# Two token tiles leave the dense dots for fetched rows of a turned u; GpSimd makes u's second half part

## What is computed

```python
s1 = jnp.einsum('thd,kd->thk', qh[:, :, 0], peer_keys1)
s2 = jnp.einsum('thd,kd->thk', qh[:, :, 1], peer_keys2)
v1, i1 = lax.top_k(s1, PEER_TOPK)
v2, i2 = lax.top_k(s2, PEER_TOPK)
cand = (v1[..., :, None] + v2[..., None, :]).reshape(-1, PEER_HEADS, PEER_TOPK * PEER_TOPK)
vals, flat = lax.top_k(cand, PEER_TOPK)
e = i1[flat // 16] * PEER_KEYS + i2[flat % 16]
g = jax.nn.softmax(vals, axis=-1)
act = jax.nn.gelu(jnp.einsum('thkd,td->thk', peer_u[e], xb))
out = jnp.einsum('thk,thkd->td', g * act, peer_v[e])
```

## Time and profile before

| | |
|---|---|
| median of 3 runs | 4723.21 us |
| the profiled execution, its span | 4720.1 us |
| TensorE (matmul) busy | 4462.5 us, 95% |
| VectorE busy | 2881.6 us, 61% |
| ScalarE busy | 1338.1 us, 28% |
| GpSimd busy | 913.8 us, 19% |
| dense dots, busy | 1454.0 us, 9216 matmuls |
| sums, busy | 1085.1 us, 6144 matmuls |
| projections, busy | 493.0 us, 3168 matmuls |
| mean granted TensorE clock | 0.965 of 2.4 GHz |

### The profile page before, as it was taken

The page is one execution under the profiler, slowest core; times in us unless marked ns, Lnnn a source line. Parts: engine busy times, 40 slices in busy tenths (PEclk is TensorE's granted clock), DMA queues, the critical chain, the costliest instruction groups (busy, mean ns, idle before and its releaser), DMA issues. The chain is left out here.

```text
span 4720.1 us, 71047 instructions
## 1 busy us (share of the span) xinstructions
PE 4462.5 (95%) x26288; PEld 2684.0 (57%) x26288; DVE 2881.6 (61%) x5144; ACT 1338.1 (28%) x1823; POOL 913.8 (19%) x982
## 2 busy tenths in 40 slices
PE   6999988999888997999999999999996999999997
PEld 2666643444555665666666666666663555555554
DVE  4456413444865454256667666665536888888885
ACT  3223213333211003224444444443222222222221
POOL 0000103322000110000000000000005656666650
PEclk8999989999978998999999999999998999999998
DMA  4543523331545562245554555555438888888881
GB/s 184 177 149 128 181 58 94 85 86 45 162 137 207 204 212 89 77 148 180 189 192 171 201 191 183 182 200 182 151 119 308 301 297 293 300 293 299 291 289 48
DMA packets 398289, 859.52 MB, mean 182 GB/s; under 512 B 42626, under 2 KB 233730, under 8 KB 389186
## 3 DMA queue, kind: packets, MB, share of 16 engines
q1 hardware_dynamic: 274786, 474.82, 30.1%
q0 software_dynamic: 78752, 283.31, 17.7%
q10 hardware_dynamic: 44480, 97.93, 5.5%
HBM read 677.90 MB, written 178.03 MB: 181 GB/s over the span
## 5 line engine op out<-in xcount | busy, mean ns | idle before, releaser
L381 PE MATMUL dot_ps<-h_parts,u_parts 128*128 128x384 f16 (+1 forms) x9216 | 1454.0, 317 | 7.9 <-PEq L2050 5.4
L381 PEld LDWEIGHTS dot_ps<-h_parts,u_parts 128*128 128x128 f16 x9216 | 893.1, 98 | 499.6 <-issue 8.6
L381 PE MATMUL totals_ps<-act_parts,v_parts 128*128 128x416 f16 x6144 | 1085.1, 340 | 36.8 <-DVE act_parts L3010 28.8
L381 PEld LDWEIGHTS totals_ps<-act_parts,v_parts 128*128 128x128 f16 x6144 | 602.1, 98 | 518.5 <-issue 33.4
L394 PE MATMUL in_ps<-h_parts_in,in_parts 128*128 128x384 f16 (+1 forms) x3168 | 493.0, 318 | 4.7 <-DVE in_parts L721 4.5
L2686 DVE SCALAR_TENSOR_TENSOR u_parts<-u_chunks,units,u_parts 128x1024 f16<-128x1024 f32 x126 | 161.8, 1284 | 517.6 <-ACT u_parts L2470 517.6
L2479 ACT ACTIVATE gelu<-dot_ps,units 128x384 f32<-128x384 f32 (+1 forms) x384 | 216.3, 564 | 804.1 <-PE dot_ps L381 803.6
L394 PEld LDWEIGHTS in_ps<-h_parts_in,in_parts 128*128 128x128 f16 x3168 | 309.4, 98 | 182.3 <-DVE in_parts L721 4.6
L3097 POOL DMA_INDIRECT row_value<-tmp_g_rows,row_g x256 | 305.2, 1192 | 394.0 <-POOLq L2344 316.2
L2945 ACT ACTIVATE v_parts<-v_group,units 128x1024 f16<-128x1024 f32 x128 | 136.9, 1138 | 772.7 <-PE totals_ps L381 740.1
L3104 POOL DMA_INDIRECT rows_in<-in_v,row_v x204 | 285.8, 1401 | 229.9 <-DVE row_sums L3040 98.5
(11 more groups left out here) (371 smaller groups left out, 5294.2 us busy)
## 6 DMA issues: line engine op xcount, KB each, us to landing
u_chunks<-in_u SPq DMA_DIRECT2D x128, 512.0 KB, 5.6
v_sweep<-in_v SPq DMA_DIRECT2D x128, 512.0 KB, 4.7
v_group<-in_v SPq DMA_DIRECT2D x31, 2048.0 KB, 8.4
tmp_g<-gelu ACTq DMA_DIRECT2D x128, 416.0 KB, 2.7
tmp_w<-h POOLq DMA_DIRECT2D x26, 2048.0 KB, 8.1
w_groups<-tmp_w SPq DMA_DIRECT2D x32, 1664.0 KB, 11.7
gelu_in<-tmp_g SPq DMA_DIRECT2D x31, 1664.0 KB, 8.9
merge_sweep<-in_u POOLq DMA_DIRECT2D x64, 512.0 KB, 7.8
```

Of the source, the lines that this page charges most:

```text
L381: mm = pe.matmul(bank, left(x), right(y), start=first and x == 0 and y == 0, stop=last and x == 1)
```

## The change

1. The last 256 tokens (two blocks of 128) leave the dense dots; these now run over 832 tokens in two parts of 416 (DSPLITS), in two PSUM banks.
2. For them u is needed with an expert's 1024 values in one row. While u chunks lie in the sweep buffers of the projections (64) and of the join (64), TensorE turns each by eight transposes (two fills of four, class Turned), ScalarE copies a fill from PSUM and stores the rows to tmp_u_rows. The projections have one bank for fills and the ring of two; the join two banks and a ring of four, with a query weight chunk in a ring of its own.
3. In the dots GpSimd fetches 256 times a row of u for each of 128 tokens (a ring of four), and VectorE multiplies it with the token's h and sums along it in one instruction; h of the two blocks is turned by 16 transposes at the start. At the end one gelu and one product make the coefficients, so g_rows, its 256 value fetches and their products go.
4. The second f16 part of u moves to GpSimd, as a plain subtraction; for that ScalarE scales the f32 chunk in place with a second instruction.
5. The expert choice for the two blocks starts in the queries (the first 16 of each key half, ten searches per query chunk); their tiles come first. 128 chunks are now 8 ahead, 16 more, 6 turns of 16, 8 behind, and the last 16 one-hot groups run beside the last 8.
6. The maxima of v move: 64 into the projections, 36 beside the v product, 28 into the queries. Stores of w move from GpSimd's queue to ScalarE's.

```diff
+class Turned:
+    FILLS = 2
+    def __init__(self, nc, ctx, sem, name, a, s, sweep, banks):
+        self.a, self.s, self.sweep, self.banks = a, s, sweep, banks
+        self.rows = ctx.enter_context(nc.sbuf_tensor(name + "_rows", [P, 2, D], F32))
+        self.turned, self.taken = sem(name + "_turned"), sem(name + "_turn_taken")
+        self.stored = [sem(f"{name}_rows_out{r}") for r in range(2)]
+    def load(self, pool, n, src):
+        if n >= self.sweep.ring:
+            pool.wait_ge(self.turned, (n - self.sweep.ring + 1) * self.FILLS)
+        self.sweep.load(pool, n, src)
+    def tensor(self, pe, turn, per, k, fill):
+        at = k * self.FILLS + fill
+        if fill == 0:
+            self.sweep.wait_loaded(pe, turn, per, k)
+        pe.wait_ge(self.taken, turn * (per * self.FILLS) + at + 1)
+        bank = self.banks[at % len(self.banks)]
+        src = self.sweep.buf[k % self.sweep.ring]
+        for j in range(4):
+            col = (fill * 4 + j) * P
+            mm = pe.transpose(bank[:, j * P:(j + 1) * P], src[:, col:col + P], self.s["const"][:, C_ID:C_ID + P])
+        mm.then_inc(self.turned, 1)
+    def scalar(self, act, turn, per, k, fill, first=0):
+        at, slot = k * self.FILLS + fill, k % 2
+        if fill == 0:
+            act.wait_ge(self.stored[slot], turn * (16 * per // 2) + 16 * (k // 2 + 1))
+        act.wait_ge(self.turned, turn * (per * self.FILLS) + at + 1)
+        act.copy(self.rows[:, slot, fill * 512:(fill + 1) * 512],
+                 self.banks[at % len(self.banks)]).then_inc(self.taken, 1)
...
+        LATE_SWEEP = CH_G // RING - CH_X // RING
+        sweep = Sweep(nc, ctx, sem, "proj", s["u_tops"], 2, [s["rstd"][:, 0:KC * P]])
+        v_sweep = Sweep(nc, ctx, sem, "proj_v", s["v_tops"], 2)
+        to_rows = Turned(nc, ctx, sem, "proj", a, s, sweep, [ps_v[:, :]])
         with nc.Block() as block:
             @block.gpsimd
             def _(pool):
-                sweep.gpsimd(pool)
+                for n in range(SWEPT):
+                    to_rows.load(pool, n, a["u"][n].rearrange("p k e -> p (k e)"))
+                    v_sweep.load(pool, n, a["v"][n // GRP, :, n % GRP, :])
+                for n in range(V_STEPS, V_STEPS + V_TAIL):
+                    v_sweep.load(pool, n, a["v"][n // GRP, :, n % GRP, :])
             @block.sync
             def _(sp):
...
+                            if swept is not None and k % 2 == 0:
+                                to_rows.tensor(pe, swept, PASS, 2 * u + k // 4, k // 2 % 2)
                         if u == 1 and not last:
                             scales.turn(pe, i + 1)
                         if u == 2 and not last:
...
-                def take(i, func, row0, dest, last=False):
-                    act.wait_ge(unit_ready, i + 1)
+                def take(i, func, row0, dest, swept, last=False):
                     for u in range(RING):
                         b = u % 2
+                        for f in range(2 * Turned.FILLS):
+                            to_rows.scalar(act, swept, PASS, 2 * u + f // 2, f % 2)
+                        if u == 0:
+                            act.wait_ge(unit_ready, i + 1)
...
+                def passing(swept, us, vs):
+                    for k in us:
+                        sweep.vector(dve, swept, PASS, k)
+                    for k in vs:
+                        v_sweep.vector(dve, swept, PASS, k)
                 def turn(i, work=None, swept=None):
                     set_unit(i)
                     found(i + 1)
                     if work:
                         work(0)
+                    if swept is not None:
+                        for k in range(4):
+                            passing(swept, (k,), (k,))
                     scales.powers(dve, link.link, i + 1)
                     if work:
                         work(1)
+                    if swept is not None:
+                        passing(swept, (4, 5), (4, 5))
                     take_scales(i + 1)
-                    for u in range(3):
-                        split(i + 1, u)
-                        if swept is not None:
-                            for k in range(2):
-                                sweep.vector(dve, swept, 2 * u + k)
+                    split(i + 1, 0)
+                    split(i + 1, 1)
+                    if swept is not None:
+                        passing(swept, (6,), ())
+                    split(i + 1, 2)
+                    if swept is not None:
+                        passing(swept, (7,), ())
                     if work:
                         work(2)
                     split(i + 1, 3)
                     if swept is not None:
-                        for k in range(2):
-                            sweep.vector(dve, swept, 6 + k)
+                        passing(swept, (), (6, 7))
                     if work:
                         work(3)
...
+                assert SWEPT == V_STEPS == (last + 1) * PASS
+                for k in range(PASS):
+                    passing(last, (k,), (k,))
                 for t in range(TILES + 1):
                     n = min(P, T - t * P)
...
                     dve.tensor_tensor(s["dt_tok"][0:n, t, :], ps_dt[0:n, 0:SH],
                                       s["par"][0:n, W_DTB:W_DTB + SH], ALU.add).then_inc(dt_taken, 1)
+                    for k in range(4):
+                        v_sweep.vector(dve, 0, PASS, V_STEPS + t * 4 + k)
...
-        EACH = 5
-        sweep = Sweep(nc, ctx, sem, "merge", a, s, SWEPT, NK - SWEPT, EACH, [], 2 * EACH, range(2 * EH))
+        PASS = 4
+        sweep = Sweep(nc, ctx, sem, "merge", s["u_tops"], PASS)
+        query_sweep = Sweep(nc, ctx, sem, "merge_query", s["u_tops"], 1)
+        turn_ps = ctx.enter_context(nc.psum_tensor("merge_turn_ps", [P, 2, 512], F32))
+        to_rows = Turned(nc, ctx, sem, "merge", a, s, sweep, [turn_ps[:, b, :] for b in range(2)])
         with nc.Block() as block:
             @block.gpsimd
             def _(pool):
-                sweep.gpsimd(pool)
+                for n in range(SWEPT):
+                    to_rows.load(pool, n, a["u"][SWEPT + n].rearrange("p k e -> p (k e)"))
+                    if n % PASS == PASS - 1:
+                        c = n // PASS
+                        query_sweep.load(pool, c, a["w_query"][c].rearrange("p k e -> p (k e)"))
...
+                def turn_fill(step, at):
+                    to_rows.tensor(pe, step, PASS, at // Turned.FILLS, at % Turned.FILLS)
                 group[0].tensor(pe)
                 group[1].tensor(pe)
                 pe.wait_ge(o_in, 16)
...
                                           start=(k == 0), stop=(k == NA - 1))
+                            turn_fill(i * 2 + u, j)
                         if u == 0:
                             pe.wait_ge(y_ready, KC)
                         for j, (t0, n) in enumerate(SPLITS):
                             for k in range(KC):
                                 mm = pe.matmul(ps[:, NS + j, 0:n], wb[:, u, k, :], y[:, k, t0:t0 + n],
                                                start=(k == 0), stop=(k == KC - 1))
+                                if k == 3:
+                                    turn_fill(i * 2 + u, NS + 2 * j)
                             mm.then_inc(br_done, 1)
+                            if j < NS - 1:
+                                turn_fill(i * 2 + u, NS + 2 * j + 1)
                 pe.wait_ge(br_taken, KC * NS)
...
                                                start=(k == 0), stop=(k == KC - 1))
+                                if k in (1, 4) or k == 6 and j < NS - 1:
+                                    turn_fill(i * 2 + (KC + u), 3 * j + (1, 4, 6).index(k))
                             mm.then_inc(mix_done, 1)
                 norm.tensor(pe)
...
+                        to_rows.scalar(act, i, PASS, at // Turned.FILLS, at % Turned.FILLS, SWEPT)
                 act.wait_ge(mix_taken, KC + 2)
                 norm.scalar(act)
                 shifted(act, s, h, 3 * KC, h_scaled)
+                to_rows.end(act, SWEPT)
             @block.vector
             def _(dve):
                 link = Chain(dve, chain)
...
+                def passing(step):
+                    for k in range(PASS):
+                        sweep.vector(dve, step, PASS, k, SWEPT)
+                    query_sweep.vector(dve, step, 1, 0, NK)
                 dve.sem_inc(mix_taken, 2)
                 for g in range(NG):
...
-                        for k in range(EACH):
-                            sweep.vector(dve, i, EACH * u + k)
+                        passing(i * 2 + u)
...
-                        for k in range(EACH):
-                            sweep.vector(dve, i + KC // 2, EACH * u + k)
+                        passing(i * 2 + (KC + u))
...
+                def rest(at):
+                    r = (at.n + 2) % 4
+                    pool.wait_ge(u_hi, at.chunk(off=3))
```

(36 more changed lines are left out.)

## The result

The changed kernel takes 4802.5 us, the median of four runs (4783.9 to 4807.5), against 4723.7 us of the kernel before beside it: 1.016 times as long, with an interval of 1.014 to 1.018. It is slower, as forecast. The time is 60 us above the predicted 4742, inside the range. A second set of four runs gave 4796.0 us (ratio 1.016, 1.014 to 1.018). The first profiled execution was the fastest of its set, 4783.9 us; that of the second set, 4796.4, is the typical one. Both are read here.

What follows compares the result with a forecast made beforehand. TensorE was taken to bound the projections, join, dots and sums. 4720.1 - 335 (dots) + 118 (transposes) + 62 (projections) + 24 (their end) + 109 (join) + 29 (clock) + 12 (small terms) = 4739; median 4742 us, range 4640 to 4870.

Steps and rivals of the forecast that it cites:

- Transposes +118: Projections and join: 256 fills of four transposes at 0.46 us add 118 us to TensorE, half in each.
- Join +109, clock apart: Join: TensorE waits for ring refills, 8.4 us at seven branch steps and 6.4 at eight output steps, 109 us.
- Rival 1: Projections and join: loads land in time, rings don't hold TensorE; 4542 us, 4645 with half the stalls; chance 0.20.
- Projections +62: Projections: new TensorE waits of 3.9, 2.3 and 0.9 us a turn, and 15 us in turn 7; sum 62 us.
- the clock: Half clock after TensorE stalls: 1.7 us a restart, 15 in the join and two in the projections, +29 us.
- Rival 3: Join: the clock stays low, two fifths of it at 1.2 GHz, +120 us, 4870 us; chance 0.08.
- End of the projections +24: After the input products: 36 v maxima through two slots, paced by landings at 3.14 us each, add 24 us.
- Dots -335: Dots: a chunk's dense matmuls fall from 11.03 to 8.41 us, over 128 chunks saving 335 us.
- VectorE: 114 of 150 us: Dots: VectorE's work per turn goes from 109 to 114 us, within a turn of 150 us.
- rival 4: Dots: VectorE's rows come late, a row product twice as dear, 154 of 150 us a turn; +40, 4790 us; chance 0.04.
- rival 2: Dots: GpSimd becomes the bound; 4790 us at 6 us a subtraction, 4980 at 8 us; chance 0.14.
- To the dots +4, to the sums +8: Small terms: token transposes 2 and VectorE's searches 2; end of the dots 4 and five row fetches 4 us.

Runs made afterwards that it cites:

- e1_join_first: The changed kernel with VectorE taking a step's five maxima ahead of its additions in the join, not behind: 4652.9 us, 0.985 of the kernel before.
- e3_v_ring4: The changed kernel with four slots instead of two in the projections' ring for v's chunks: 4759.3 us, 1.008 of the kernel before.
- e4_proj_order: The changed kernel with some u and v maxima moved earlier in VectorE's order in a projection turn: 4738.5 us, 1.003 of the kernel before.
- e6_vector_sub: The changed kernel with u's second part made by VectorE again in the dots, without GpSimd's subtraction and ScalarE's scaling in place: 4781.9 us.
- e8_old_pool_sub: The kernel before with only GpSimd's subtraction, ScalarE's scaling in place and w's stores on ScalarE's queue: 4729.0 us, ratio 1.0013.

## Why the prediction was right, and where its sizes were off

**What bounds the kernel, and the sign: right.** The ring of the join refilled behind the step (146 us) and the transposes (55 in the join, as many by estimate in the projections) take back 256 of the 310 us that the dense cut gave; the rest made it slower. `e1_join_first` shows the cause of the sign directly: with TensorE's waits in the join gone the change pays, which neither `e3_v_ring4` nor `e4_proj_order` reaches alone.

**Transposes +118.** 0.46 us a fill from the rows of another phase, 0.43 measured in the join: right. In the projections a fill wasn't measured by itself.

**Join +109, clock apart.** Measured 105.9 and 108.3, 15 times, 9.1 us the longest. The chain of the step (VectorE's order, issue, landing) was right in each link; the waits are 7.1 us each in the mean where 7.3 were forecast. Rival 1 (rings that don't hold TensorE) is out with them.

**Projections +62.** The sum of waits is 61.9 us (35.2 + 19.5 + 7.2), but its make-up is not that of the prediction. A turn has one wait of 5.1 to 6.4 us, not three of 3.9, 2.3 and 0.9: the load took 7.7 us to land instead of the 4.8 of the earlier trace rows, and the second wait hid behind the first until `e3_v_ring4` brought it out. The load goes out among the store of the banks, a weight chunk and two v loads; that they make it late wasn't tried. Turn 7 cost 10.9, not 15. Errors of either sign met in a sum that looks exact.

**The step that failed most in the projections is the clock.** Only two restarts were priced there; the other waits were forecast at 0.9 to 3.9 us, below the 4.62 of the earlier trace rows. The seven that came were 4.8 to 6.4 us, and `e4_proj_order` gives back some 14 us beyond the waits. In the join it is 33 (first execution) to 37 us (second) where 25.5 stood: a restart costs 2.0 (projections) to 2.5 us, not 1.7. Together the clock came to some 50 us where 29 stood, which with the shorter fills makes up the +9 and +7 of the two stretches. Rival 3 (a join that stays low) is out: the windows show 0.86 to 0.89, and 1.00 without the waits.

**End of the projections +24.** 32 measured. The pace was right: the 36 maxima run from 733.6 to 843.2 us, 3.0 us each for the 3.14 of the earlier trace rows, and `e3_v_ring4` shows that landings set it. The start was missed: VectorE first waits for the first tile's dt sums, so its first maximum comes 9 us after the last input product:

```profile
724.76 7.03 PE L672 MATMUL v_ps<-wv,h 128*128 128x512 f32 x16
...
733.64 2.35 DVE L324 TENSOR_REDUCE v_tops<-proj_v_sweep 128x1 f32<-128x1024 f32 x2
```

**Dots -335.** The largest miss, 25 us. The arithmetic of the dense cut held: where chunks run without one-hots, 286 matmuls take 50 us, so 48 take 8.4 us. The window, and then TensorE's timeline at about the start of the loop's second round:

```profile
2500.00:2550.00 50.00, 50.00 (x286) 27.86 (x285) 37.85 (x138) 20.42 (x24) 32.19 (x21) 1.00 0.81 256
```

```profile
2911.87 6.07 PE L437 MATMUL dot_ps<-h_parts,u_parts 128*128 128x416 f16 x24 [3.58 <-issue]
```

What was left out is idle time of TensorE before w_ps and dot_ps: about 10 us for right, another 10 named issue (6.1 + 4.4; 4.0 + 6.8 in the second execution; 9.6 in `e6_vector_sub`), more than half of it at the start of the loop's second and third rounds in the first execution, which no edit removed and whose cause wasn't tried, and the half clock behind some of both (24 matmuls in 6.07 us, not 4.38). The step that failed is "VectorE: 114 of 150 us" with every instruction at its undisturbed time: VectorE was busy 87 of 100 us, not 76. The mechanism had been named, in the sentence on the Trainium skill and in rival 4, but priced as nothing since it was looked for as a wait for u_parts. It came as a longer one-hot. The prediction tied that contention to rival 2, and wrongly: the contention is there and rival 2 is out, since the subtraction takes 2.41 us, well under 3.9, and 2.15 in `e8_old_pool_sub`. The 2.2 us estimated from the page GPSIMD Engine Reference of the Trainium skill (section Elementwise — side-by-side cycle accounting) lies between the two. Rival 4 came in part: a row product took 1.53 us, not 1.28 and not twice that, and VectorE waited 88 us for rows.

**To the dots +4, to the sums +8.** 10.9, and 10.7 and 11.7, measured. TensorE waits 11.6 us at the queries' end (5.4 before), while VectorE does the last searches and v maxima, and the 16 token transposes take 3.3. At the sums' start the first pair of w and gelu is there 17.4 us after the first load is issued, against 11.6 before; the five row fetches now go out beside those loads, as the prediction had it, but it gave them 4 us, not 6. That they are the cause wasn't tried.

**Sums 0.** They gained 9 us: the wait of 8.0 us at their start in the kernel before, for VectorE's additions into h, is gone (0.4 after). The value fetches and their products, which the prediction called hidden, ran just there; that their going is the cause wasn't tried. It is the one term in the change's favour.

The sum of the misses in the second execution: 9 + 9 + 3 + 7 + 7 + 25 + 4 - 9 + 1 = 56 us, which is the distance from 4739 to 4794.7.

## What to carry to other kernels

When a new consumer joins a ring that was only swept before, go through every engine's queue for what stands ahead of the instruction that frees a slot: here the same transposes and loads cost 146 us more when five maxima stand behind a step's additions than when they stand before them. Price each wait of a full TensorE at its length plus the clock behind it, and take a landing from a moment with the same traffic. Work moved from VectorE to GpSimd must be charged to both, since an instruction with two SBUF inputs can stand still until the other engine's is over (3.15 us instead of 1.22 here); count it where VectorE's own lateness would be felt.

## What the runs showed of the hardware

- Beside GpSimd's two-input subtraction (2.41 us for 128x1024, 2.15 with VectorE less busy) VectorE's row products and one-hots, with two inputs, took 1.50 to 1.74 us in the mean instead of 1.22, and single ones 3.15; the searches (FIND_INDEX8) stayed at 0.27 to 0.29 us. GpSimd's 305 us of work made VectorE's other work 181 us longer.
- An idle TensorE of 4.8 to 8.8 us cost 2.0 to 2.5 us more by the half clock after it (37 us behind 15 waits in the join, where the same 1520 matmuls took 408 instead of 372 us; 14 behind seven in the projections).
- Four 128x128 f32 transposes between full-rate matmuls cost 0.43 us, though their own row shows 0.60.
- A product with a sum along the row over 128x1024 f32 (the row product) takes 1.22 us with a second instruction of 0.08 that reads the accumulator, less than the 1.28 of a scaled subtraction over the same tile.
- A 512 KB load landed after 3.7 to 7.9 us in the kernel before, and a stage's median hides it: 4.8 was the median of a stage before the change, 5.0 that of the same buffer's loads after it, and the load that TensorE waited for took 7.7.
